# Down projection of a hybrid decoder layer: seven Strassen-Winograd products walked in another order, with weight sums carried in place

## The reference, cut to what matters

```
    up = h @ w_up
    ...
    gate, val = jnp.split(conv, 2, axis=-1)
    y = (jax.nn.gelu(gate) * val) @ w_down
...
    f, conv_new = _conv_ffn(_rmsnorm(x, lw['g_ffn_pre']), conv_prefix, lw['w_up'], lw['w_conv'],
                            lw['b_conv'], lw['w_down'])
    x = x + _rmsnorm(f, lw['g_ffn_post'])
    gate = jax.nn.sigmoid(_rmsnorm(x, lw['g_ple_in']) @ lw['w_ple_gate'])
    x = x + _rmsnorm((p @ lw['w_ple']) * gate, lw['g_ple_post'])
```

## Time and profile before

| what | value |
|---|---|
| median of the runs | 2571.89 us (2564.39 to 2572.33) |
| the profiled execution | 2567.34 us |
| its span | 2565.6 us |
| TensorE busy | 2450.7 us, 96% |
| VectorE, ScalarE, GpSimd busy | 63%, 43%, 29% |
| bytes moved | 446.36 MB, 174 GB/s over the span |
| down projection | about 1812 to 2308 us of the span |

### The profile page before, as it was taken

How to read it: one execution, slowest core, us unless ns; L and a number is a source line. 1 busy time by engine, 2 the same in 40 slices (tenths; PEclk the granted TensorE clock), 3 DMA queues, 4 the chain that set the end, 5 groups by cost and what they waited for, 6 DMA issues and landing times. The chain is left out here.

```text
span 2565.6 us, 37984 instructions
## 1 busy us (share of the span) xinstructions
PE 2450.7 (96%) x13790; PEld 2200.8 (86%) x13790; DVE 1609.7 (63%) x2342; ACT 1099.2 (43%) x2005; POOL 733.2 (29%) x925
## 2 busy tenths in 40 slices
PE   8999999989999799999999999999899999969998
PEld 6789999977877699999999999999687888757887
DVE  4301232278786488889888899888556667674332
ACT  4311111145454466666666666665322323243232
POOL 1100001035565322234334454444100002342222
PEclk9999999989899899999999999999999999989999
DMA  5213778674334456554656545653779989972221
GB/s 174 92 58 111 241 228 262 216 192 133 109 125 126 136 178 201 177 167 144 203 186 195 166 136 184 210 181 128 186 223 276 260 215 308 273 247 98 92 74 45
DMA packets 478522, 446.36 MB, mean 174 GB/s; under 512 B 67666, under 2 KB 372626, under 8 KB 478328
## 3 DMA queue, kind: packets, MB, share of 16 engines
q1 hardware_dynamic: 478348, 444.10, 56.6%
HBM read 330.07 MB, written 113.95 MB: 173 GB/s over the span
## 5 line engine op out<-in xcount | busy, mean ns | idle before, releaser
L2646 PE MATMUL up_chain<-up_bh,up_ah 128*128 128x348 f32 (+1 forms) x1056 | 342.8, 325 | 16.3 <-DVE up_up L2498 7.3
L2646 PE MATMUL up_chain<-up_bh,up_al 128*128 128x348 f32 (+1 forms) x1056 | 340.7, 323 | 0.0
L2646 PE MATMUL up_chain<-up_bl,up_ah 128*128 128x348 f32 (+1 forms) x1056 | 340.4, 322 | 0.0
L2511 DVE SCALAR_TENSOR_TENSOR up_conv<-up_up,ffn_features,up_conv 128x696 f32<-128x696 f32 (+1 forms) x264 | 255.6, 968 | 61.6 <-ACT up_conv L2319 51.3
L3519 PE MATMUL down_acc<-down_bh,down_ah 128*128 128x512 f32 x616 | 245.7, 399 | 33.0 <-DVE down_al L3291 18.5
L2199 POOL TENSOR_TENSOR up_conv<-up_conv 128x696 f32<-128x696 f32 (+1 forms) x66 | 132.4, 2006 | 430.4 <-DVE up_conv L2511 300.0
L3519 PE MATMUL down_acc<-down_bh,down_al 128*128 128x512 f32 x616 | 242.7, 394 | 0.0
L3519 PE MATMUL down_acc<-down_bl,down_ah 128*128 128x512 f32 x616 | 242.6, 394 | 0.0
L2434 DVE TENSOR_TENSOR up_al<-up_sums,up_ah 128x512 fp32r<-128x512 f32 x256 | 228.1, 892 | 7.0 <-ACT up_ah L2252 6.9
L2646 PEld LDWEIGHTS up_chain<-up_bh,up_ah 128*128 128x128 f32 x1056 | 200.1, 190 | 20.3 <-DVE up_up L2498 9.6
L2434 DVE TENSOR_TENSOR up_al<-up_raw,up_ah 128x512 fp32r<-128x512 f32 x192 | 186.4, 971 | 42.5 <-ACT up_ah L2252 42.5
(11 more groups left out here) (378 smaller groups left out, 6210.4 us busy)
## 6 DMA issues: line engine op xcount, KB each, us to landing
up_sums<-weight_sums SPq DMA_DIRECT2D x256, 256.0 KB, 4.0
up_raw<-in_w_up SPq DMA_DIRECT2D x64, 512.0 KB, 5.0
down_araw<-hidden SPq DMA_DIRECT2D x36, 704.0 KB, 6.8
in_up_raw<-in_w_up SPq DMA_DIRECT2D x44, 512.0 KB, 7.3
weight_sums<-in_up_sum SPq DMA_DIRECT2D x22, 1024.0 KB, 5.7
down_araw<-diffs SPq DMA_DIRECT2D x32, 704.0 KB, 8.0
down_keep<-in_w_down SPq DMA_DIRECT2D x77, 256.0 KB, 5.6
up_raw<-in_w_up SPq DMA_DIRECT2D x64, 256.0 KB, 3.4
```

Source lines behind the costliest of these rows:

```text
L2511: last = nc.vector.scalar_tensor_tensor(out=out[:, 0:n], in0=up[g % 2][kind][:, c:c + n], in1=out[:, 0:n], scalar=taps[:, f, c:c + 1], op0 ...
L2646: last = nc.tensor.matmul(acc[:, 0:HALF[p]], a[:, q % RING, k, :], b[:, m - 1, k, left(p)], start=(opens and k == 0 and i == 0), stop=(k = ...
```

## The change

The walks come in the order 1, 2, 7, 6, 4, 5, 3. Three walks in a row then go on from each other's weights: walk 7 multiplies by 22 - 12, walk 6 by that plus 11, walk 4 by 21 minus that. So walk 6 adds 11 to what walk 7 left in `keep[k]`, and walk 4 subtracts `keep[k]` from 21; t2 isn't stored or loaded any more. Walk 5 loads 12 and 11 anew, walk 3 loads 22. Of 12 weight blocks per chunk (1 + 1 + 3 + 2 + 2 + 2 + 1) 9 are left (1 + 1 + 2 + 1 + 1 + 2 + 1), each with at most one addition. `b_sums` waits, where nothing is loaded into `keep[k]`, for the split of the walk before.

On the output side the products 6 and 7 and the products 4 and 5 change places. Walk 7 now writes `w` = bank + `u`; walk 6 adds its bank to `w` and to `u` (two operations per tile); walk 4 makes the staged right half from bank + `w`; walk 5 adds its bank to `w` and to `u` and completes the right rows. `FINISHED` therefore holds walk 5's steps (two blocks of hidden per tile) in place of walk 4's (one block). The rest of the diff follows from that (4 becomes 5 where the finishing walk is meant, 5 becomes 4 where the staged one is).

```diff
-WALKS = (1, 2, 6, 7, 5, 4, 3)
+WALKS = (1, 2, 7, 6, 4, 5, 3)
...
-B_PARTS = {1: ("11",), 2: ("21",), 6: ("22", "12", "11"), 7: ("22", "12"), 5: ("12", "11"), 4: ("21", "t2"), 3: ("22",)}
-B_SIGNS = {6: (ALU.subtract, ALU.add), 7: (ALU.subtract,), 5: (ALU.subtract,), 4: (ALU.subtract,)}
+B_KEPT = {1: "11", 2: "21", 7: "22", 5: "12", 3: "22"}
+B_ADDED = {7: "12", 6: "11", 4: "21", 5: "11"}
 A_PARTS = {1: ("e1",), 2: ("o1",), 6: ("o2", "de"), 7: ("de",), 5: ("e2", "o2"), 4: ("o2",), 3: ("do", "de")}
 A_SIGN = {6: ALU.subtract, 5: ALU.add, 3: ALU.add}
-FINISHED = [step for step in DOWN_STEPS if step[0] in (4, 3)]
+FINISHED = [step for step in DOWN_STEPS if step[0] in (5, 3)]
...
 B_CHUNKS = [(v, k) for v in range(len(WALKS)) for k in range(PAIRS)]
-B_TEMPS = [(v, k, part) for v, k in B_CHUNKS for part in B_PARTS[WALKS[v]][1:]]
+B_TEMPS = [(v, k) for v, k in B_CHUNKS if WALKS[v] in B_ADDED]
 B_TEMP_AT = {b: n for n, b in enumerate(B_TEMPS)}
+
+
+def kept_loads(v):
+
+    return 16 * sum(1 for m in WALKS[:v + 1] if m in B_KEPT)
...
             def load_b(v, k):
-                parts = B_PARTS[WALKS[v]]
-                if v > 0:
-
-                    sp.wait_ge(wready, chunk_at(v - 1, k) + 1)
-                    if WALKS[v - 1] == 6:
-                        sp.wait_ge(t2_stored, 16 * PAIRS)
-                sp.dma_start(keep[:, k, :], b_source(k, parts[0])).then_inc(keep_in[k], 16)
-                for part in parts[1:]:
-                    n = B_TEMP_AT[v, k, part]
+                m = WALKS[v]
+                if m in B_KEPT:
+                    if v > 0:
+
+                        sp.wait_ge(wready, chunk_at(v - 1, k) + 1)
+                    sp.dma_start(keep[:, k, :], b_source(k, B_KEPT[m])).then_inc(keep_in[k], 16)
+                if m in B_ADDED:
+                    n = B_TEMP_AT[v, k]
                     if n < 4:
                         sp.wait_ge(tail_stored[n], 32 * len(range(n, groups, 4)))
                     else:
                         sp.wait_ge(b_summed, n - 3)
-                    sp.dma_start(temps[n % 4], b_source(k, part)).then_inc(temp_in[n % 4], 16)
-
-            def store_t2(k):
-                sp.wait_ge(b_summed, b_sums_to(chunk_at(WALKS.index(6), k)))
-                sp.dma_start(t2_rows[k], keep[:, k, :]).then_inc(t2_stored, 16)
+                    sp.dma_start(temps[n % 4], b_source(k, B_ADDED[m])).then_inc(temp_in[n % 4], 16)
...
                         load_b(v, k)
-                for v, k in summed_at(i):
-                    if WALKS[v] == 6:
-                        store_t2(k)
                 for gr in tail_groups(i - 1):
                     store_tail(gr)
-                if i >= 1 and DOWN_STEPS[i - 1][0] in (2, 5):
+                if i >= 1 and DOWN_STEPS[i - 1][0] in (2, 4):
...
                 c = chunk_at(v, k)
-                if len(B_PARTS[WALKS[v]]) > 1:
+                if WALKS[v] in B_ADDED:
                     act.wait_ge(b_summed, b_sums_to(c))
                 else:
-                    act.wait_ge(keep_in[k], 16 * (v + 1))
+                    act.wait_ge(keep_in[k], kept_loads(v))
...
             def b_sums(v, k):
-                c = chunk_at(v, k)
-                dve.wait_ge(keep_in[k], 16 * (v + 1))
-                for part, sign in zip(B_PARTS[WALKS[v]][1:], B_SIGNS.get(WALKS[v], ())):
-                    n = B_TEMP_AT[v, k, part]
-                    dve.wait_ge(temp_in[n % 4], 16 * (n // 4 + 1))
-                    if n >= 1:
-                        dve.wait_ge(b_summed, n)
-                    nc.vector.tensor_tensor(keep[:, k, :], keep[:, k, :], temps[n % 4], sign).then_inc(b_summed, 1)
+                if (v, k) not in B_TEMP_AT:
+                    return
+                m, n, mine = WALKS[v], B_TEMP_AT[v, k], keep[:, k, :]
+                if m in B_KEPT:
+                    dve.wait_ge(keep_in[k], kept_loads(v))
+                else:
+
+                    dve.wait_ge(wready, chunk_at(v - 1, k) + 1)
+                    dve.wait_ge(b_summed, b_sums_to(chunk_at(v - 1, k)))
+                dve.wait_ge(temp_in[n % 4], 16 * (n // 4 + 1))
+                if m == 4:
+                    nc.vector.tensor_tensor(mine, temps[n % 4], mine, ALU.subtract).then_inc(b_summed, 1)
+                else:
+                    nc.vector.tensor_tensor(mine, mine, temps[n % 4], ALU.add if m == 6 else ALU.subtract)\
+                        .then_inc(b_summed, 1)
...
                     nc.vector.tensor_tensor(y[tile % 2][:, 0:512], bank[:, :], mine, ALU.add).then_inc(emptied, 1)
-                elif m in (6, 3):
+                elif m == 3:
                     nc.vector.tensor_tensor(mine, bank[:, :], mine, ALU.add).then_inc(emptied, 1)
                 elif m == 7:
                     nc.vector.tensor_tensor(w_tile(tile), bank[:, :], mine, ALU.add).then_inc(emptied, 1)
-                elif m == 5:
+                elif m == 4:
                     staging_free(m, tile)
-                    nc.vector.tensor_tensor(y[tile % 2][:, 0:512], bank[:, :], w_tile(tile), ALU.add)
+                    nc.vector.tensor_tensor(y[tile % 2][:, 0:512], bank[:, :], w_tile(tile), ALU.add).then_inc(emptied, 1)
+                else:
+                    nc.vector.tensor_tensor(w_tile(tile), bank[:, :], w_tile(tile), ALU.add)
                     nc.vector.tensor_tensor(mine, bank[:, :], mine, ALU.add).then_inc(emptied, 1)
-                else:
-                    nc.vector.tensor_tensor(w_tile(tile), bank[:, :], w_tile(tile), ALU.add).then_inc(emptied, 1)
...
                     dve.wait_ge(right_stored[s], 16 * (SAMPLE // 2))
-                halves = (w_tile(tile), half[s]) if m == 4 else (half[s], u[:, tile, :])
+                halves = (half[s], w_tile(tile) if m == 5 else u[:, tile, :])
```

## The result

| | before | after |
|---|---|---|
| median of the runs | 2565.24 us (2561.80 to 2572.33, 5 runs) | 2587.45 us (2586.01 to 2588.69, 5 runs) |
| span of the profiled execution | 2565.6 us | 2585.9 us |
| bytes moved | 446.36 MB | 434.81 MB |

The change makes the kernel slower, by under 1%: ratio 1.0075, 95% interval 1.0063 to 1.0087. (The ratio is estimated from the single runs, so it isn't the quotient of the two medians.) The sign was forecast, and the time lies in the range (2564 to 2596), but the loss is 20.3 us between the two profiled executions where the sum said 9.8.

The account below looks back on a forecast made before the run. TensorE was taken as the bound, busy 2450.7 of 2565.6 us, with full DMA costing much only in walk 3. 2567.3 - 3.9 + 12.3 + 1.4 = 2577.1 us, about half of 4.6 added for a median: 2580, range 2564 to 2596.

Parts of the forecast that it names:

- the sum: All terms together for an execution like the profiled one: 2577.1 us, +9.8.
- (1): Fewer weight blocks: TensorE's waits at walk 6 and in walk 5 go, -3.9 us, bounds 0 and -3.9.
- (2): VectorE: eleven sums fewer and eight emptyings more, both beside matmuls: 0 us.
- the third price of step (3): VectorE's own work in the finishing walk: three rounds of 10.3 us with a sum and second emptying, 8.4 over TensorE's.
- (3): Finishing moves from walk 4 to walk 5, with two blocks of hidden per tile: +12.3 us, bounds 4.7 and 20.
- (4): Matmuls at a slower clock after a long wait, counted once: +1.4 us, bounds 0 and 5.
- The forecast itself: Walk 5 pays 8 to 17 us, total 2575 to 2584 us; chance 0.6.
- rival C: Walk 5 becomes a second walk 3, paying 20 us and the clock 5: 2591 us; chance 0.1.
- A: DMA engines keep up: walk 5 pays 4.7 us or less, -3.9 cancels it, 2566 to 2570; chance 0.2.
- B: Walk 3's 11.17 us wait, after seven weight blocks queued in one burst, goes: -10.4, 2559 us; chance 0.1.
- The signs to look for: Walk 5 at 68 to 77 us, waits for al 1.5 to 4 each, splits 18 to 20 apart, DMA share near 1.

Follow-up runs that it names:

- e7: The kernel before, with the staged half loaded ahead of hidden and the next phase's 13 weight blocks loaded two to a round: 2566.37 us, ratio 0.9996.
- e9: The kernel before, with the loads of hidden for the sample's step of walk 3 cut from 11 weight pairs to 3: 2567.19 us, ratio 1.0000.
- e10: The kernel before, with the sample's short step second in walk 3 instead of fifth: 2565.39 us, ratio 0.9991.
- e11: e7 with the sample's step second in walk 3: 2562.59 us, ratio 0.9981.
- e4: The changed kernel without VectorE's sum of the two blocks of hidden in walk 5, the first block alone being used: 2584.53 us, ratio 1.0072.
- e2: The changed kernel, with x1 and the staged half loaded ahead of hidden in each SyncE round: 2573.31 us, ratio 1.0030.
- e5: e2 with the next phase's 13 weight blocks loaded two to a round instead of seven in one burst: 2573.66 us, ratio 1.0027.
- e6: e2 with walk 3's weight blocks and x1 for walk 5's rows loaded to a quarter of their columns: 2565.26 us, ratio 0.9994.
- e8: The changed kernel's weight sums, but rows finished in walk 4 as in the kernel before, with both edits of order of e5: 2567.88 us, ratio 1.0002.

## Why the prediction was right in sign and half the size

*(1) Waits that go, -3.9.* Right: no wait is left in walks 7, 6 and 4, and walk 6 and the staging walk are 6.7 us shorter between the two profiles. How much that is varies among executions: in e7, e9, e10 and e11, which have the old order of walks, walk 6 takes 66.4 to 69.6 us, where the new order has 64.9 each time. The term lies inside that spread. The sum left out waits under 0.9 us and gaps that aren't listed as waits.

*(2) VectorE, 0.* Right, and e4 shows it for the sums of walk 5 too, where the third price of step (3) had put 8.4 us on the sums and the second emptying.

*(3) The finishing moves, +12.3.* **This is the step that failed.** The place was right (al from the fourth tile on, SyncE behind, the half last), and so were the two mechanisms, loop and bytes. Three prices were worked out, and the text took "the bytes' 12.3 us, which lies between the other two", as if they were three readings of one loss. The runs show losses that add: 8.1 us that the loop takes, 9.4 that 5.3 MB take, and 6.5 that neither edit removes. The bytes' price by itself wasn't far off: in e2, where the engines are full, walk 5 takes 14.9 us more than walk 4 took before (75.17 less 60.23), slow matmuls included. What failed is that the loop's 8.1 us were taken to lie inside it; they come on top. Waits in walk 5 measure 18.1 us where 12.3 stood.

*(4) The clock, +1.4.* Too small: one such time was counted, of 1.4 us, and walk 5 has two, after its two longest waits, 3.9 us in all. The rows it was read from had more as well: the earlier trace rows shows three waits of walk 3 "each followed by slow matmuls", of which one stretch was priced.

*The sum.* -6.7 + 23.0 + 0.7 for walk 3 is +17.0; the other 3.3 us of the 20.3 lie outside the stretch that the change touches.

*The range.* It holds 2587.45 because it was drawn wide enough for rival C. The forecast itself does not: walk 5 was to pay 8 to 17 us, 2575 to 2584, and it pays 23.0. (In the chances two thirds of 0.6 and C's 0.1 make 0.50 and not 0.53; nothing else hangs on it.)

*The rivals.* A (DMA keeps up) falls: 5.3 MB less were needed to come near it. No walk 5 that finishes rows passed 296 GB/s (in e5). Both figures of the Trainium skill ("DMA: Bandwidth & Descriptors", Specifications) that rival A weighs, 435 and about 358, lie above that. B (the burst) falls twice: the wait stayed at 10.97 us, and the burst wasn't its cause. C, walk 5 as a second walk 3 at 20 us and a clock of 5, is nearest by its price: walk 5 pays 23.0 with the clock in it, and its rows read like walk 3's. It had 0.1 against 0.6, because walk 3's pace was put down to a burst that walk 5 doesn't have; e5 shows that walk 3 keeps its pace without the burst (100.44 us, 100.57 in e2).

*The signs to look for.* Walk 5 took 83.26 us, not 68 to 77, and two of its five waits are over the 4 us that were given. From the fourth tile on, splits two tiles apart came out at 20.3 to 26.2 us, not 18 to 20. Walk 5 had a share of 0.96 at 267 GB/s. Near 1 was to mean bytes and under 0.9 the loop; the loop was there at 0.96 all the same, so the share alone doesn't tell them apart. Nor do the GB/s: e6, in which the half stands first, moves 265 at a share of 1.01.

## What to carry to other kernels

Where a stage can be slowed in two ways, by a full resource and by a chain of releases, work both out and ask whether one hides the other; here they added, and only the crossed pair of edits showed it. Bytes that lie beside matmuls in a stage without waits are worth little, while a finishing step that is moved into a stage with double loads pays for everything its transfers queue behind. In a queue that issues in written order, the small transfer on which other engines wait goes first where the stage loses by that wait; in a stage that hides it (walk 4 in e7 and e8) the same edit gained nothing.

## What the runs showed of the hardware that was not expected

VectorE's split takes 1.61 us alone and, beside GpSimd's addition of x1, up to 2.9 us in walk 5 and 3.5 in walk 3. In the turn shown above GpSimd's row is

```profile
2181.93 2.66 POOL L3467 TENSOR_TENSOR down_y<-down_y,down_res 128x1024 f32<-128x1024 f32 x1 [1.59 <-DVE down_y L3376]
```

It ends at 2184.59, and the split that starts at 2183.50 ends 1.48 us after that; the emptying at 2182.90, which reads one operand from PSUM, keeps its 0.68 us in the same time. The eight splits of walk 5 take 17.7 us instead of 12.9. This is no loss that the change brought: in walk 4 of the kernel before the eight splits take 18.3 us, and TensorE waits for none of them. The Trainium skill ("SBUF — State Buffer", SBUF: two separate sides) says that a GpSimd operation that reads SBUF and a VectorE operation with two SBUF inputs take a shared pair of ports in turn, each for its whole instruction, and the one that comes second waits; this trace agrees, to 0.13 us (1.48 after the addition's end, 1.61 alone).

And SyncE's issue itself can become a wait. In walk 5 of the changed kernel the two loads of hidden for one tile, 704 KB each, took 1.04 us to issue near the walk's start and 4.34 us later:

```profile
2138.63 1.04 SPq L3014 DMA_DIRECT2D down_araw<-hidden  x2
...
2171.09 4.34 SPq L3014 DMA_DIRECT2D down_araw<-hidden  x2
```

During the first the DMA engines moved 3 GB/s, at a share of 0.03; during the second 282 GB/s, at 1.08. That the longer issue comes from engines that still have work is argued from these stretches; no run was made for it. Whatever stands behind in that queue is late by it, though no semaphore shows it.
